# Reciprocals in three parts, and a new place for sixteen value rounds, in an attention and linear-attention decoder layer

## What is computed

```python
# prompt, in 128-query blocks; c is the running sum of the log-forget values
s = q @ k.T * scale + c[q] - c[k]          # masked to the past
o = softmax(s) @ v

# samples: eight tokens, cached rows fetched by a page table
k_all = concat(cache_k[page_table], k); v_all = concat(cache_v[page_table], v)
s = q @ k_all.T * scale + c[past] - c
o = softmax(s) @ v_all
```

## Time and profile before

| | |
|---|---|
| median of three executions | 1752.76 us (1752.53 to 1757.63) |
| the profiled execution | 1749.94 us, its span 1748.2 us |
| PE busy | 1690.8 us (97% of the span) |
| DVE, ACT, POOL busy | 806.2, 420.1, 750.0 us |
| granted TensorE clock, mean | 0.980 |

### The profile page before, as it was taken

One profiled execution on the slowest core, in us unless ns is written; L12 is line 12 of the kernel. 1 busy time (PEld: TensorE's weight loads), 2 busy tenths in 40 slices (PEclk: granted clock), 3 DMA queues, 4 the chain that ended last, 5 costly groups with the idle time before them and its releaser, 6 DMA issues.

```text
span 1748.2 us, 28804 instructions
## 1 busy us (share of the span) xinstructions
PE 1690.8 (97%) x11472; PEld 1580.6 (90%) x11472; DVE 806.2 (46%) x1284; ACT 420.1 (24%) x764; POOL 750.0 (43%) x584
## 2 busy tenths in 40 slices
PE   7999999998999899999999999999999999999995
PEld 7978787876888899999999989999999999999994
DVE  4157767651324251111264758535534533542527
ACT  4033333332334351111020642110110011011133
POOL 4310111101112203333244646976786686686325
PEclk9899999998999999999999999999999999999998
DMA  5244444413653021111112221211121121121302
GB/s 163 63 110 130 111 142 128 139 28 110 193 159 74 7 69 49 47 38 47 48 44 78 61 73 34 69 51 43 55 61 37 49 67 32 49 67 44 91 25 97
DMA packets 180298, 130.25 MB, mean 75 GB/s; under 512 B 30842, under 2 KB 153050, under 8 KB 180050
## 3 DMA queue, kind: packets, MB, share of 16 engines
q1 hardware_dynamic: 174546, 127.24, 25.1%
q10 hardware_dynamic: 5632, 1.35, 0.4%
HBM read 117.63 MB, written 10.92 MB: 74 GB/s over the span
## 4 chain that ended last, share of the span: by engine, by line
PE 84%; DVE 8%; ACT 2%; issue 2%; DMA 2%; SPq 1%; POOL 1%; DVEq 0%; ACTq 0%; POOLq 0%
PE psum L1667 7%; PE psum L1660 7%; PE psum L1666 7%; PE psum L1005 5%; PE psum L1008 5%; PE psum L1009 5%; PE psum L1727 4%; PE psum L1731 4%; PE psum L1730 4%; PE psum L1066 4%; PE psum L1070 4%; PE psum L1072 4%; PE psum L1232 3%; PE psum L1562 3%; PE psum L1566 3%; PE psum L1565 3%
## 5 line engine op out<-in xcount | busy, mean ns | idle before, releaser
L868 POOL CAST wh<-raw 128x1024 fp32r<-128x1024 f32 x72 | 87.8, 1219 | 766.2 <-PE psum L1066 373.4
L870 POOL TENSOR_TENSOR wl<-raw,wh 128x1024 fp32r<-128x1024 f32 x72 | 190.2, 2641 | 5.8
L898 POOL TENSOR_TENSOR wl<-raw,wh 128x512 fp32r<-128x512 f32 x126 | 168.9, 1341 | 10.1
L1066 PE MATMUL psum<-xh,wh 128*128 128x352 f32 (+1 forms) x480 | 162.8, 339 | 2.3 <-DVE ql L2445 2.3
L1070 PE MATMUL psum<-xl,wh 128*128 128x352 f32 (+1 forms) x480 | 163.3, 340 | 0.0
L1660 PE MATMUL psum<-xh,wh 128*128 128x258 f32 x576 | 162.5, 282 | 0.0
L1072 PE MATMUL psum<-xh,wl 128*128 128x352 f32 (+1 forms) x480 | 162.4, 338 | 0.0
L1666 PE MATMUL psum<-xl,wh 128*128 128x258 f32 x576 | 162.4, 282 | 0.0
L1667 PE MATMUL psum<-xh,wl 128*128 128x258 f32 x576 | 162.2, 282 | 0.0
L3040 DVE TENSOR_TENSOR mixed<-mixed,psum 128x344 f32<-128x344 f32 x216 | 108.3, 510 | 74.6 <-PE psum L1731 74.4
L1727 PE MATMUL psum<-hh,wh 128*128 128x344 f32 x432 | 138.6, 321 | 0.2
(11 more groups left out here) (396 smaller groups left out, 4380.1 us busy)
## 6 DMA issues: line engine op xcount, KB each, us to landing
raw<-in_w_in SPq DMA_DIRECT2D x86, 256.0 KB, 3.4
parts<-in_cache_k SPq DMA_DIRECT2D x64, 256.0 KB, 3.0
parts<-in_cache_v SPq DMA_DIRECT2D x64, 256.0 KB, 2.9
raw<-in_w_gate SPq DMA_DIRECT2D x44, 256.0 KB, 2.9
raw<-in_w_up SPq DMA_DIRECT2D x44, 256.0 KB, 2.9
raw<-in_w_down SPq DMA_DIRECT2D x44, 256.0 KB, 2.9
raw<-in_w_o SPq DMA_DIRECT2D x28, 256.0 KB, 3.1
cb<-negc_scratch SPq DMA_DIRECT2D x8, 520.0 KB, 5.3
```

What stands on the lines that cost most here:

```text
L1066: ins = mm(out, wt(wh, slot, k), xh[:, k, c0:c0 + cw], start=(k == 0), stop=False)
```

## The change

The reciprocal of a segment's sums is cut into pieces of 128 columns (the last of a 272-column segment has 16), which DVE takes in three steps in a row, two, three and four steps behind the segment's end, each after both places of the maxima; the multiplication follows the third. Value rounds 0 and 1 stand at x = 14 and 17 of the last pair, rounds 2 to 15 are put among the chunks and transposes behind the attention, and the output of a sample comes one chunk or round after the round that DVE has to mask. FRONT_PART becomes 7, and SP's panels 21 to 23 go out one round earlier by number. The wait of PE for the last copy of the mix (o_copied) moves from before the first chunk to before the gate logits.

```diff
--- before.py
+++ after.py
@@ -205,14 +205,14 @@
 
 KEYS_AT = [3 + 50 * c // PARTS for c in range(PARTS)]
 SUMS_AT = {8: (1, 2), 10: (3,), 11: (4,), 13: (5,)}
-ROUNDS_AT = {14: 0, 15: 1, 16: 2, 17: 3}
+ROUNDS_AT = {14: 0, 17: 1}
 ROUNDS = 2 * NB
 FRONT = {"gate": [3, 4, 2], "logits": [6, 7, 5], "q": [5, 2, 3], "k": [4, 7, 6], "v0": [5, 2, 3], "kt": [6, 7, 6],
          "vt0": [7, 6, 7], "v1": [4, 5, 2], "vt1": [6, 7, 6]}
 
 
 
-FRONT_PART = 11
+FRONT_PART = 7
 VALUE_PLACE = []
 for c_ in range(PARTS):
     VALUE_PLACE.append(c_ if c_ < 3 else 3 if c_ == FRONT_PART else VALUE_PLACE[c_ - (3 if c_ < FRONT_PART else 4)])
@@ -662,8 +662,8 @@
                     for c in range(2 * ROUNDS_AT[x] + 3, 2 * ROUNDS_AT[x] + 5):
                         values_part(c)
             values_part(FRONT_PART)
-            for r in range(4, ROUNDS):
-                p = {4: 21, 6: 22, 9: 23, 12: 24}.get(r)
+            for r in range(2, ROUNDS):
+                p = {3: 21, 5: 22, 8: 23, 12: 24}.get(r)
                 if p is not None:
                     panel(p, column_of(p))
                 for c in range(2 * r + 4, min(2 * r + 6, PARTS)):
@@ -1339,9 +1339,7 @@
                     for u in SUMS_AT.get(x, ()):
                         sample_sums(u)
                 fill()
-            sample_outputs(0)
             pe.wait_ge(sem("probs_ready"), 2 * STEPS * 4)
-            pe.wait_ge(sem("o_copied"), 4 * SEGS * 4)
 
             def gate_logits(i, banks):
                 pe.wait_ge(sem("params_loaded"), 16 * 7)
@@ -1357,44 +1355,48 @@
                     pass
             G0 = PAN_GLA + GH
             whole(G0 - 1, 0, "gate")
+            sample_outputs(0)
+            value_round(2)
+            pe.wait_ge(sem("o_copied"), 4 * SEGS * 4)
             gate_logits(0, FRONT["logits"])
             whole(G0 - 1, 1, "gate")
+            value_round(3)
+            whole(G0 - 1, 2, "gate")
             value_round(4)
             sample_outputs(1)
-            whole(G0 - 1, 2, "gate")
+            whole(G0, 0, "q")
             value_round(5)
-            whole(G0, 0, "q")
+            whole(G0, 1, "q")
             value_round(6)
             sample_outputs(2)
-            whole(G0, 1, "q")
+            whole(G0, 2, "q")
             value_round(7)
-            whole(G0, 2, "q")
+            whole(G0 + 1, 0, "k")
             value_round(8)
             sample_outputs(3)
-            whole(G0 + 1, 0, "k")
+            whole(G0 + 1, 1, "k")
             value_round(9)
-            whole(G0 + 1, 1, "k")
+            whole(G0 + 1, 2, "k")
             value_round(10)
             sample_outputs(4)
-            whole(G0 + 1, 2, "k")
+            whole(G0 + 2, 0, "v0")
             value_round(11)
-            whole(G0 + 2, 0, "v0")
+            whole(G0 + 2, 1, "v0")
             value_round(12)
             sample_outputs(5)
-            whole(G0 + 2, 1, "v0")
+            whole(G0 + 2, 2, "v0")
             value_round(13)
-            whole(G0 + 2, 2, "v0")
-            value_round(14)
-            sample_outputs(6)
             for b in FRONT["k"]:
                 settled(b)
             turn((ke,), FRONT["kt"], [])
-            value_round(15)
+            value_round(14)
+            sample_outputs(6)
             for b in FRONT["v0"]:
                 settled(b)
             whole(G0 + 3, 0, "v1")
+            value_round(15)
+            whole(G0 + 3, 1, "v1")
             sample_outputs(7)
-            whole(G0 + 3, 1, "v1")
             whole(G0 + 3, 2, "v1")
             turn((gvT,), FRONT["vt0"], [(gvT,)])
             for b in FRONT["v1"]:
@@ -2498,10 +2500,14 @@
                         if i % PER_SEG == PER_SEG - 1 and n == len(pieces(i)) - 1:
                             max_split(p, i // PER_SEG)
 
-            def outputs(j, s):
+            def outputs(j, s, third):
                 n = min(SEG, TP - SEG * s)
-                dve.wait_ge(sem("o_copied"), 4 * (SEGS * j + s + 1))
-                link(ve.reciprocal(sums_of[:, 0:n], sums_of[:, 0:n]))
+                if third == 0:
+                    dve.wait_ge(sem("o_copied"), 4 * (SEGS * j + s + 1))
+                cols = slice(P * third, min(P * third + P, n))
+                link(ve.reciprocal(sums_of[:, cols], sums_of[:, cols]))
+                if third < 2:
+                    return
                 o = o32[:, j, SEG * s:SEG * s + n]
                 ve.tensor_tensor(o, o, sums_of[:, 0:n], ALU.mult)\
                     .then_inc(sem("o_read"), 1)
@@ -2592,11 +2598,11 @@
             for g in range(-STEPS, 4 * STEPS + 2):
                 j, x = divmod(g, STEPS)
                 maxima_at(j, x, 0)
-                if g >= 2:
-                    j2, x2 = divmod(g - 2, STEPS)
-                    if x2 in SEG_END:
-                        outputs(j2, SEG_END.index(x2))
                 maxima_at(j, x, 1)
+                for third in range(3):
+                    j2, x2 = divmod(g - 2 - third, STEPS)
+                    if j2 >= 0 and x2 in SEG_END:
+                        outputs(j2, SEG_END.index(x2), third)
                 if j < 3:
                     for u in range(len(UNITS)):
                         if UNIT_DONE[u] == x:
@@ -2614,8 +2620,10 @@
                         own_scores()
                     for u in SUMS_AT.get(x, ()):
                         sums(u)
-                    if x == 16:
+                    if x == 17:
                         own(0)
+            outputs(3, 2, 1)
+            outputs(3, 2, 2)
             own_out(0)
             own(1)
```

## The result

The changed kernel took 1740.96 us (median of four executions, 1728.26 to 1741.22) beside 1753.8 us for the kernel before (median of four): a ratio of 0.9915, interval 0.9889 to 0.9941. The forecast was 1739.6 us, the range 1734 to 1748. Timed twice more, six executions each beside the kernel before, the changed kernel had ratios of 0.9934 (0.9918 to 0.9949) and 0.9948 (0.9930 to 0.9966). So it is faster by 0.5 to 0.85%, and the first measurement is the upper end of that. In microseconds the three timings give 12.8, 11.8 and 9.6 us, where 13.2 were forecast. The profiled execution took 1741.12 us, its span 1739.4, against 1749.94 and 1748.2 before.

A forecast was written before the change was run, and what follows sets the result against it. PE, busy 97% of the span, bounds the kernel; time returns only from its waits and lower clock. 11.2 + 2.0 = 13.2 us off 1749.94 gives 1736.7, or 1739.6 us against the median; range 1734 to 1748.

The forecast's parts named there:

- part 1: Value rounds moved: removes waits of rounds 1 to 3, 6.2 us, and slow-clock loss behind them, 5.0; together 11.2 us.
- gain in pair 0, steps 5 and 6: Shorter reciprocal before the maxima takes 2.1 us off PE's 2.61 us wait; full clock behind it returns 1.7 us.
- the three small waits: Remaining three of PE's six waits for DVE's maxima in the attention, 1.0 us in all, counted as gone.
- (a): Last piece in next pair's step 3 delays ACT's copies; PE's mix waits 0.2 to 0.7 us, together 1.2 us lost.
- (b): Step 6, pairs 0 to 2: last piece and multiplication precede the joined maxima; PE waits about 0.3 us each, 1.0 lost.
- (c): Step 5 of pair 1: second piece, 0.94 us, lands before the key part ahead of the 1.40 us wait; 0.6 lost.
- from round 4 on the pace is the one at which no wait shows: Later value rounds take 5.9 or 5.0 us each, parts asked for two rounds ahead, so no load wait.
- A wait is paid twice: PE loses the idle time, then runs at half clock behind it; behind the rounds' waits 5.0 us of work lost.
- One of the signs of being wrong: Waits of over 2 us for ACT's copies or DVE's maxima in pairs 1 to 3 would show the forecast wrong.
- Part 2: Reciprocals cut and spread in the attention: 4.8 us gained, 2.8 lost to new waits, 2.0 us net.
- The price of a start: Each reciprocal on DVE costs 0.14 us to start; 24 more pieces cost 3.4 us of DVE time.
- The first rival: Cut reciprocals only pay: part 2 gives nothing to a loss of 2.5 us, time 1741.6 to 1744.1; chance 0.18.

The follow-up runs named there:

- the rounds alone: Changed kernel with the whole reciprocals back in their old place, so only the value rounds are moved; 1740.89 us, ratio 0.9936.
- the filled waits: Kernel before with useless matmuls in the waits ahead of rounds 2 and 3: 1748.51 us; with more, also before the first chunk: 1749.97 us.

## Why the prediction was right, and where not

The sign, the time and the range held. That the median came within 1.4 us of the forecast is in part luck: the profile gained 13.0 us in the two parts, but two other profiles of the same kernel gained only 9.1 and 9.2 us there, and what the untouched code takes moves by 9 us. By its steps, taking each step of the attention by the time between its start and the next one's:

| step of the prediction | said, us | measured (after against before), us |
|---|---|---|
| part 1, from pair 3's step 14 to the recurrence | 11.2 | 10.8 (profile), 10.4 (profile of the rounds alone), 11.2 (timed alone, interval 7 to 15) |
| gain in pair 0, steps 5 and 6 | 2.1 + 1.7 | 2.35 + 1.19 = 3.54 |
| the three small waits | 1.0 | 1.3: pair 0 0.68, pair 2 0.71 less 0.49, pair 1 0.43 |
| (a) mix at step 4 of pairs 1, 2, 3 | 0.25, 0.7, 0.25 | 0.25, 0.91, 0.26 |
| (b) step 8 of pairs 0, 1, 2 | 0.3 each | 0.29, 0.29, 0.26 |
| (c) pair 1, steps 5 and 6 | 0.6 | 0.22 + 0.17 |

**Part 1** went as worked out. Rounds 1, 2 and 3 have no idle time ahead, the clock stays at 1.00, and no round from 4 to 13 waits. The begin of the recurrence kept its cover: DVE's last work on the samples' output ended 0.8 us before PE came (507.84 and 508.65), what the prediction had left. What it missed is round 14: it follows round 13 after 489.51 - 486.68 = 2.8 us, not 5.0, because only transposes stand between them, and waits 0.23 us (0.6 and 0.9 in the two other profiles of this kernel). A term of the prediction, "from round 4 on the pace is the one at which no wait shows", took all gaps to be alike. "A wait is paid twice" held by the filled waits, with limits on both sides: the clock also fell with no wait over 0.84 us left, and once with none, and it stayed up behind a wait of 2.76 us. One of the signs of being wrong, a wait of over 2 us for DVE's maxima in pairs 1 to 3, is there (2.60 us in pair 1). It is the wait that the prediction itself left standing at 2.36 us, so the sign was badly chosen.

**Part 2**: all three losses are there with their mechanisms. The one of (a) can be followed in the kernel after (timelines of DVE and ACT; PE's mix is in the fence above, at 280.64):

```profile
277.76 0.24 DVE L2508 RECIPROCAL sums_of<-sums_of 128x16 f32<-128x16 f32 x1
278.04 0.44 DVE L2512 TENSOR_TENSOR o<-o,sums_of 128x272 f32<-128x272 f32 x1
```

```profile
278.57 0.49 ACT L1957 ACTIVATE o<-psum 64x384 f32<-64x384 f32 x1 [1.93 <-DVE o L2512]
...
280.10 0.48 ACT L1959 ACTIVATE sums_of<-psum 64x384 f32<-64x384 f32 x1
```

The last piece and the multiplication end at 278.5, ACT's first copy begins at once, its fourth ends at 280.6, and PE's mix starts then. The price of a start was right too. All reciprocals of the kernel after by form (count, busy us, mean ns), against the earlier trace rows:

```profile
L2508 DVE RECIPROCAL sums_of<-sums_of 128x128 f32<-128x128 f32 x32 | 30.3, 946 | 6.1 <-ACT sums_of L1959 6.1
...
L2508 DVE RECIPROCAL sums_of<-sums_of 128x16 f32<-128x16 f32 x4 | 1.0, 248 | 0.0
```

31.3 us in place of 8 x 2.545 + 4 x 1.844 = 27.7: 3.6 us more for 24 pieces, 3.4 said. The Trainium skill's rule on small tiles ("VectorE: DVE Perf Modes", the section on the TRN2 errata) is borne out in that cost, and the estimate from its figure, 3.7 us, was as near; but only about 2.6 us of (a) to (c) fell on PE's path, and the spread brought more than that.

**The step that failed** is a silence: "The waits of 2.36 and 1.40 us ... leave ... 1.0 us for the other three, which I count as gone" took one of these three, 0.19 us at step 12 of pair 1, as gone for good. It is a wait behind DVE's wait for the row `cb`, which the score blocks of the next pair need and which SP sends off 2 us before step 11. Timelines of DVE and PE in the kernel before:

```profile
240.03 0.30 DVE L2475 CUSTOM_DVE_ANT_0 psum<-psum,cb 128x128 f32<-128x128 f32 x1 [2.08 <-DMA cb<-negc_scratch]
...
240.69 0.38 PE L1162 MATMUL psum<-kh,qh 64*128 64x256 f32 x2 [0.19 <-DVE nmax L2475]
```

Timeline of DVE and the DMA issues between 225 and 245 us (KB each, median us from issue to landing) of the kernel after:

```profile
237.75 0.30 DVE L2477 CUSTOM_DVE_ANT_0 psum<-psum,cb 128x128 f32<-128x128 f32 x1 [1.74 <-DMA cb<-negc_scratch]
```

```profile
cb<-negc_scratch SPq DMA_DIRECT2D x2, 520.0 KB, 5.0
```

and of the changed kernel again (timelines of DVE and PE, DMA issues between 225 and 245 us):

```profile
239.41 0.30 DVE L2477 CUSTOM_DVE_ANT_0 psum<-psum,cb 128x128 f32<-128x128 f32 x1 [3.81 <-DMA cb<-negc_scratch]
```

```profile
240.07 0.39 PE L1162 MATMUL psum<-kh,qh 64*128 64x256 f32 x2 [1.68 <-DVE nmax L2477]
```

```profile
cb<-negc_scratch SPq DMA_DIRECT2D x2, 520.0 KB, 6.4
```

Where the row's two loads land 1.4 us later in the median, and DVE reads it 2.1 us later in the step, PE waits 1.68 us, the clock falls at 241.4 for 3.4 us, and step 12 takes 8.05 us in place of 4.51 (4.94 before). Of the three profiles of the changed kernel, two have it (87.62 and 87.49 us for pair 1), and then part 2 loses 1.1 to 1.2 us instead of gaining 2.2. So "part 2 gives 2.0" is right for the first profile of the changed kernel and too much for the two others; with the timed ratios, part 2 beside part 1 is worth between some 4 us and a loss of 2. The first rival, that the cut reciprocals only pay, had the size for those executions, but not the mechanism: pair 0 gained 3.9 us in all five profiles with the spread. Whether the spread makes the row late is open. SP issues it 2.0 us before step 11 in all these profiles. Without the spread it is read 3.8 to 5.5 us after that step's begin (five profiles), with it 5.7 to 6.1 in four and 3.9 in one. In the four late ones the loads just ahead of it are late as well: the key load sent off 0.4 us before it landed after 4.4 to 5.1 us, against 2.9 in the kernel after; the latest of the five without the spread has 4.1 us there. So more than this one row is slow then. A second place for the row, asked for earlier, would tell; it was not tried.

## What to carry to other kernels

Spread work that waits for loads until each load has a chunk or two of other work ahead of it; the matmuls stay the same, and the wait and the slow clock behind it both go. When a long instruction on a helper engine stands before what the main engine waits for, put its pieces into different steps, not merely cut it, and place each by who is queued behind it. A small wait for a load is a chance, not a constant: look at it in more than one profile before counting it as gone. And on a queue that is served in order, loads that nobody waits for yet delay the row behind them: the pages made a query row late in pair 1 and, moved, another one in pair 2.

## What I had not expected of the hardware

The granted clock fell with PE busy for 14.00 of 14 us, behind matmuls of one and eight columns and sixteen rows, in one of the ten profiles that hold this group in this order; the cause is open. It stayed at full behind a wait of 2.76 us in one profile, and fell for 3.4 us behind one of 0.91 us in the same one. Stretches at half clock of 3.4 and 6.8 us come and go in untouched code, and an execution's time moves by 1.5 us with each 3.4. A load of 520 KB, issued at the same point of the program, landed after 5.0 us in one execution and 6.4 in another of the same kernel (median of its two halves).
